# A merge gate whose last four weight tiles go bank by bank, with the merged tile's transposes among them and inside the second output projection

## The chip, the core and the metric

The kernel runs on one core of a Trainium2 chip. Its engines work side by side and meet only at semaphores: TensorE (PE) multiplies and accumulates into PSUM banks, ScalarE (ACT) applies activations and copies, VectorE (DVE) does elementwise work, GpSimd (POOL) as well, and SyncE (SP) issues the transfers. The metric is the device time of one execution in microseconds, lower is better; a kernel is given by the median of its runs.

## The reference

Two transformer blocks stand one after the other on 256 tokens of width 1024. The change lies in the second block, where two branches are gated and added, and the sum goes through an output projection:

```python
merged = jax.nn.sigmoid(g_a) * o_gla + jax.nn.sigmoid(g_b) * o_sgu
y = jnp.einsum('bte,ed->btd', merged, w_out[l])
x = x + gate1[:, None, :] * y
h2 = modulate(rms_norm_2(x, norm2_w[l]), shift2, scale2)
y2 = peer(h2, peer_w_q[l], peer_keys1[l], peer_keys2[l], peer_down[l], peer_up[l])
```

`g_a` and `g_b` are slices of one input projection `h @ w_in`; `o_gla` is the output of the gated linear attention, `o_sgu` that of the spatial gating unit. `peer` retrieves experts with a query projection `w_q`.

## The kernel before

All products are computed in float32 quality from two rounded parts. Each weight tile of 128 x 1024 goes through three engines: SP loads it into `raw` (`tile`, L326), ACT copies it rounded into `whi` (`hi`, L493), POOL subtracts to get the remainder `wlo` (`lo`, L431), and PE multiplies with both. There are four slots for each of the three (R = 4), and tile n uses slot n % 4. So the `hi` of tile n waits until PE has finished with tile n - 4 (`tile_used`) and the transfer of tile n has landed (`raw_full`); the `lo` waits for the `hi`; PE waits for the `lo`; and the transfer of tile n + 4 waits for the `lo` of tile n. ACT and POOL take the tiles strictly in order, with other work written between them by hand.

The second block's projections run as groups of eight tiles (k = 0 to 7), one for each 128 of the 1024 inputs. `m_tile` (L855) multiplies one tile into the four banks 0 to 3: bank b holds tokens 128 * (b // 2) onward and half b % 2 of the 1024 outputs, so a tile takes three matmuls for each bank (L867, L868, L869), twelve in all. The group `m_gb` computes `g_b` from the tiles called k0 to k7 below. `m_group_by_halves` runs the first six of them over all banks, then k6 and k7 over banks 0 and 1, then k6 and k7 over banks 2 and 3. As each bank is complete, ACT takes the sigmoid in place (L763), DVE multiplies by `msu` (L1767) and adds into `go` (L1768), the merged tile: two halves of 128 tokens, each of 1024 columns.

`go` must be transposed before the next product. PE transposes 128 x 128 blocks (`transposes`, L923), sixteen in all, into banks 4 to 7; the eight of the first 128 tokens stand ahead of the last tile of `m_gb` on banks 2 and 3, the eight of the other tokens after the group. Bank 4 + b then holds the inputs for tiles 2b and 2b + 1 of the next group: ACT copies it rounded into `xh` (`upper`, L523) and DVE subtracts to get `xl` (`turned`, L1309).

The group `wout2` is the output projection, from the tiles called w0 to w7 below (`m_group_by_halves` with the last three by halves: w0 to w4 over all banks, then w5 to w7 over banks 0 and 1, then over banks 2 and 3). DVE multiplies each finished bank by `gate1` (L1780) and adds into `xres` (L1783), between them it works on the conditioning tiles (`ada_tile`, L1344 and L1346), ACT and POOL make the norm, DVE scales (L1785), and PE transposes again (L923) and goes on to the query projection (`f_tile`, L849 to L851).

The order in which each engine meets its work is written out by hand. On ACT, around the change:

```python
his(T_IN2_M + 40 + 3, T_WOUT2 + 2)
...
    if b == 1:
        upper_of(T_WOUT2 + 2, T_WOUT2 + R - 1)
upper_of(T_WOUT2 + R - 1, T_WOUT2 + R)
upper("merged_T", first=4)
his(T_WOUT2 + R, T_WQ)
```

So ACT rounds w0 and w1 ahead of the first sigmoid, w2 after the second, w3 after the fourth, and only then the transposed banks. POOL's order is plain: `root` of the attention's norm (L450, L452) stands between k2 and k3, and from there on k3 to k7 and w0 to w7 follow each other.

Of the kernel before, what the change touches and what calls it, by code (L numbers as in the profile page):

```python
# [14 lines left out]
P = 128  # L15
# [38 lines left out]
def acc_freed(group, bank):  # L54

    before = GROUPS[:GROUPS.index(group)]
    if not before or group == "peer":
        return None
    if group == "in_M":
        return (("turned_lo", turn("mix", 4, 1)), ("gy_done", 1), ("ri_done", 1), ("ld_done", 1))[bank]  # L60
    if group == "wout":
        return (("turned_lo", turn("y", 4, 1)), ("turned_lo", turn("y", 4, 2)), ("a_raw", 6), ("a_pT", 6))[bank]
    last = before[-1]
    if last == "in2_T":
        return "xg_out", bank + 1
    if group == "merged_T":
        return "go_done", 1
    if group == "in2_T":
        return "unturned", scaled_at("in2", bank // 2 + 1)
    if last == "merged_T":  # L70
        return "unturned", scaled_at("merged", bank // 2 + 1)
    return ("turned_lo", turn(last[:-2], 4, bank + 1)) if last in TRANSPOSES else (READ_OUT[last], bank + 1)
# [22 lines left out]
Y_BANKS = [0, 1, 4, 5]  # L95

PAIRS = [(a, b) for a in range(16) for b in range(16) if (a + 1) * (b + 1) <= 16]
NPAIR = len(PAIRS)

TURNS = ["mix", "y", "mlp", "in2", "merged", "wq"]
SCALED = ["mix", "in2", "merged", "wq"]

# [11 lines left out]
def scaled_at(name, n):  # L116
    return 2 * SCALED.index(name) + n

# [24 lines left out]
def build(nc, x, stream, ada, cols, rows, lru_w, hgmask, causal, alibi, iota, walr, wup, sguw, keys, out):  # L143
    ctx = ExitStack()
    with ctx:
# [342 lines left out]
        def _(act):  # L488
# [28 lines left out]

            def upper(group, gains=None, first=0):

                for b in range(4):  # L520
                    act.wait_ge(acc_ready, acc_filled(group, b))
# [230 lines left out]
            for tt in range(TT):  # L752
                for h in range(4):
                    nc.scalar.activation(xn[:, tt, h * T:(h + 1) * T],
                                         bank[4 + 2 * tt + h // 2][:, (h % 2) * T:(h % 2 + 1) * T], ACT.Square,
                                         accum_out=gss[:, 4 * tt + h:4 * tt + h + 1]).then_inc(S("gla_ss"), 1)
            his(T_IN2_M + 40 + 3, T_WOUT2 + 2)
            for b in range(4):
                if b < 3:
                    act.wait_ge(acc_ready, acc_filled("m_gb", b))  # L760
                else:
                    act.wait_ge(tile_used, T_IN2_M + 48)
                nc.scalar.activation(bank[b][:, :], bank[b][:, :], ACT.Sigmoid).then_inc(S("gb_out"), 1)  # L763
                if b == 1:
                    upper_of(T_WOUT2 + 2, T_WOUT2 + R - 1)
            upper_of(T_WOUT2 + R - 1, T_WOUT2 + R)
            upper("merged_T", first=4)
            his(T_WOUT2 + R, T_WQ)
            upper_of(T_WQ, T_WQ + 1)
# [70 lines left out]
        def _(pe):  # L840
# [51 lines left out]

            def m_group_by_halves(a, group, twice, turned=None, before_last=lambda: None):
# [4 lines left out]
                for k in range(KC):  # L898
                    if turned and k % 2 == 0:
                        pe.wait_ge(S("turned_lo"), turn(turned, 4, k // 2 + 1))  # L900
                    if k < KC - twice:
                        tile(k, group=group if k == 0 else None)
                    else:
                        tile(k, banks=(0, 1), used=False)
                for k in range(KC - twice, KC):
                    if k == KC - 1:
                        before_last()
                    tile(k, banks=(2, 3))
# [280 lines left out]
            for tt in range(TT):  # L1189
                for h in range(4):  # L1190
# [98 lines left out]
        def _(v):  # L1289
# [13 lines left out]

            def turned(name, gains, first=0):

                for b in range(4):
                    v.wait_ge(S("turned_hi"), turn(name, 4, b + 1))
# [10 lines left out]
            def turned_shifted(group, name, gains, shifts):  # L1318

                for b in (0, 2):  # L1320
# [5 lines left out]
                    last.then_inc(S("affine"), 1)  # L1326
                turned(name, None)

            def ada_tile(n):
# [714 lines left out]
```

## Time and profile before

| | us |
|---|---|
| median of 3 runs | 1416.97 (1416.82 to 1417.31) |
| the profiled execution | 1417.1 |
| its span, first to last instruction | 1415.3 |
| outside the span | 1.8 |
| PE busy | 1369.9 (97%) |
| POOL busy | 1056.2 (75%) |
| DVE busy | 755.6 (53%) |
| ACT busy | 710.1 (50%) |
| mean granted TensorE clock | 0.987 of full speed |

A row of a timeline gives the start in microseconds from the span's start, the busy time, the engine, the line, the operation with its output and inputs, and how many instructions it merges; in brackets the idle time of the engine ahead of it and what ended that. The instructions of PE overlap, so the distance between two starts tells its pace, not the duration. A row of the stretch view gives for each engine the busy time and the number of instructions, then the granted clock as a share of full speed (1.00 is 2.4 GHz, 0.50 is 1.2 GHz), and the DMA engines' share and rate.

### The profile page before, as it was taken

What the parts mean: (1) busy time and instruction counts of PE and PEld (TensorE: products, weight loads), DVE (VectorE), ACT (ScalarE), POOL (GpSimd) and SP (SyncE); (2) the same over time, 40 slices, a digit from 0 to 9 for tenths busy, and PEclk for the clock granted to TensorE, in tenths of its full rate; (3) what the DMA queues carried; (4) which work ended last, traced back from release to release, by engine and by line L of the source; (5) the groups of instructions that cost most, each with busy time, mean ns of one, the idle gap of its engine ahead of it and who ended that gap; (6) DMA issues with size and microseconds to landing.
All of it is one profiled execution on the core that took longest, in us unless ns stands there. A gap on an engine that the chain in (4) does not pass through costs nothing.

```text
span 1415.3 us, 28941 instructions
## 1 busy us (share of the span) xinstructions
PE 1369.9 (97%) x9762; PEld 1219.6 (86%) x9762; DVE 755.6 (53%) x1616; ACT 710.1 (50%) x1129; POOL 1056.2 (75%) x469
## 2 busy tenths in 40 slices
PE   6998999999999998899999999999999999999997
PEld 6887899998877886899999999999977777788886
DVE  4655433334258526349991176666688888611113
ACT  6444555555345443435556543343355555556664
POOL 6554688886678885668888877777777777788885
PEclk9999999998999999999999999999999999999999
DMA  8443677774545456535555554444444445475552
GB/s 305 154 164 107 243 289 279 274 264 146 198 147 180 149 172 259 199 134 179 179 187 183 178 165 162 157 155 162 157 155 163 163 165 169 156 259 193 193 191 98
DMA packets 72651, 263.02 MB, mean 186 GB/s; under 512 B 8208, under 2 KB 9104, under 8 KB 72224
## 3 DMA queue, kind: packets, MB, share of 16 engines
q1 hardware_dynamic: 72608, 262.46, 53.6%
q8 instruction: 25, 0.41, 0.1%
q14 instruction: 18, 0.15, 0.0%
HBM read 259.81 MB, written 2.62 MB: 185 GB/s over the span
## 4 chain that ended last, share of the span: by engine, by line
PE 89%; DVE 5%; issue 2%; ACT 1%; POOL 1%; DMA 1%; SPq 0%; POOLq 0%; ACTq 0%; DVEq 0%
PE bank L849 14%; PE bank L867 14%; PE bank L850 14%; PE bank L851 14%; PE bank L868 13%; PE bank L869 13%; PE bank L1242 3%; DVE arena L1718 1%; DMA raw<-stream 1%; PE bank L965 1%; POOL wlo L431 1%; PE bank L1224 1%; PE bank L923 0%; DVE bank L1346 0%; PE bank L1154 0%
## 5 line engine op out<-in xcount | busy, mean ns | idle before, releaser
L431 POOL TENSOR_TENSOR wlo<-raw,whi 128x1024 fp32r<-128x1024 f32 x432 | 1041.8, 2423 | 315.5 <-ACT whi L493 312.4
L493 ACT ACTIVATE whi<-raw 128x1024 fp32r<-128x1024 f32 x432 | 455.7, 1057 | 350.9 <-PE bank L869 255.3
L849 PE MATMUL bank<-xh,whi 128*128 128x256 f32 x1600 | 462.2, 289 | 6.9 <-DVE xl L1314 4.5
L850 PE MATMUL bank<-xl,whi 128*128 128x256 f32 x1600 | 455.3, 285 | 0.0
L851 PE MATMUL bank<-xh,wlo 128*128 128x256 f32 x1600 | 455.0, 284 | 0.0
L867 PE MATMUL bank<-whi,xh 128*128 128x512 f32 x800 | 321.2, 402 | 9.7 <-DVE xl L1549 2.5
L849 PEld LDWEIGHTS bank<-xh,whi 128*128 128x128 f32 x1600 | 309.8, 194 | 12.0 <-POOL wlo L431 6.5
L868 PE MATMUL bank<-wlo,xh 128*128 128x512 f32 x800 | 313.2, 392 | 0.0
L869 PE MATMUL bank<-whi,xl 128*128 128x512 f32 x800 | 313.0, 391 | 0.0
L850 PEld LDWEIGHTS bank<-xl,whi 128*128 128x128 f32 x1600 | 310.0, 194 | 1.2
L851 PEld LDWEIGHTS bank<-xh,wlo 128*128 128x128 f32 x1600 | 309.5, 193 | 0.0
L867 PEld LDWEIGHTS bank<-whi,xh 128*128 128x128 f32 x800 | 151.1, 189 | 44.7 <-POOL wlo L431 4.9
L869 PEld LDWEIGHTS bank<-whi,xl 128*128 128x128 f32 x800 | 151.0, 189 | 32.0
L868 PEld LDWEIGHTS bank<-wlo,xh 128*128 128x128 f32 x800 | 151.2, 189 | 28.4
L789 ACT ACTIVATE arena<-bank 128x256 f32 x128 | 49.3, 385 | 180.9 <-PE bank L851 180.7
L1916 DVE TENSOR_TENSOR xl<-bank,xh 128x256 fp32r<-128x256 f32 x128 | 53.5, 418 | 143.5 <-ACT bank L816 143.5
L1901 DVE TENSOR_TENSOR xs<-bank,xs 128x768 bf16<-128x768 f32 x128 | 121.5, 949 | 0.0
L1909 DVE TENSOR_TENSOR arena<-arena,bank 128x256 f32 (+1 forms) x128 | 53.8, 421 | 102.1 <-PE bank L1242 101.9
L1899 DVE TENSOR_TENSOR ua<-xs,bank 128x512 bf16<-128x512 f32 (+1 forms) x128 | 87.0, 680 | 0.0
L1631 DVE TENSOR_TENSOR ul<-bank,uh 128x256 fp32r<-128x256 f32 x32 | 13.6, 425 | 120.2 <-ACT bank L676 120.2
L1242 PEld LDWEIGHTS bank<-xs,ua 128*128 128x128 bf16 x1536 | 51.9, 98 | 19.3 <-DVE xs L1901 15.7
L1242 PE MATMUL bank<-xs,ua 128*128 128x64 bf16 x1536 | 67.0, 194 | 0.0
(279 smaller groups left out, 1155.5 us busy)
## 6 DMA issues: line engine op xcount, KB each, us to landing
raw<-stream SPq DMA_DIRECT2D x432, 512.0 KB, 3.3
arena<-ada SPq DMA_DIRECT2D x48, 512.0 KB, 4.8
arena<-rows SPq DMA_DIRECT2D x5, 512.0 KB, 8.6
xs<-x SPq DMA_DIRECT2D x2, 512.0 KB, 4.6
arena<-rows SPq DMA_DIRECT2D x1, 1024.0 KB, 5.4
x_spill<-xs SPq DMA_DIRECT2D x1, 1024.0 KB, 6.2
xs<-x_spill SPq DMA_DIRECT2D x1, 1024.0 KB, 6.0
out<-arena SPq DMA_DIRECT2D x2, 512.0 KB, 2.6
```

The lines of the kernel that those rows point to most:

```text
L431: nc.gpsimd.tensor_tensor(wlo[:, slot, :], raw[:, slot, :], whi[:, slot, :].bitcast(F32), ALU.subtract).then_inc(lo_done, 1)
L493: nc.scalar.activation(whi[:, slot, :], raw[:, slot, :], ACT.Copy).then_inc(hi_done, 1)
L849: nc.tensor.matmul(dst, h_, xh[:, k, :], start=(k == 0), stop=False)
L850: nc.tensor.matmul(dst, h_, xl[:, k, :], start=False, stop=False)
L851: last = nc.tensor.matmul(dst, l_, xh[:, k, :], start=False, stop=(k == KC - 1))
L867: nc.tensor.matmul(bank[b][:, :], ah[:, ts], whi[:, slot, cs], start=start, stop=False)
L868: nc.tensor.matmul(bank[b][:, :], ah[:, ts], wlo[:, slot, cs], start=False, stop=False)
L869: last = nc.tensor.matmul(bank[b][:, :], al[:, ts], whi[:, slot, cs], start=False, stop=final)
L1242: last = nc.tensor.matmul(bank[6 + q % 2][:, t_ * HALF:(t_ + 1) * HALF], oneB[:, q % 2, t_, :], oneA[:, q % 2, part, t_, :], start=(part = ...
L1899: ttt(oneB[:, slot], bc(1, P), counts.to_broadcast([P, 4, P]), ALU.is_equal)
L1901: ttt(oneA[:, slot], same.unsqueeze(1).to_broadcast([P, 3, 4, HALF]), picks[:, 2:5, ts].unsqueeze(3).to_broadcast([P, 3, 4, HALF]), ALU.mu ...
L1909: ttt(dst, dst, bank[6 + q % 2][:, 0:4 * HALF].rearrange("p (t n) -> p n t", t=4), ALU.mult)\
```

## The change

PE now runs k0 to k3 over all banks, and then one bank after the other: bank 0 with k4 to k7, bank 1 with k4 to k7, bank 2, bank 3 (`m_group_by_banks`). Since a tile is given free with its last bank, k4 to k7 are given free only in bank 3. Transposes are issued in fours: tokens 0 to 127 for banks 4 and 5 ahead of bank 2, for banks 6 and 7 ahead of bank 3; tokens 128 to 255 for banks 4 and 5 ahead of the last tile in bank 3, for banks 6 and 7 between w0 and w1. `merged_out` counts the four finished pieces of `go` and takes the place of two steps of `unturned`; the banks 0 to 3 of `wout2` wait for it one by one. ACT and DVE follow: three sigmoids, w0, two transposed banks, the fourth sigmoid, w1, the other two transposed banks, w2 onward. DVE makes `xl` of the first two banks ahead of the fourth merge. Nothing is added or removed in arithmetic. The diff adds two functions that nothing calls (`upper_among`, `turned_among`); they are left out here, as are the renamings of `before_last`.

```diff
 def acc_freed(group, bank):
...
     if last == "merged_T":
-        return "unturned", scaled_at("merged", bank // 2 + 1)
+        return "merged_out", bank + 1
...
-SCALED = ["mix", "in2", "merged", "wq"]
+SCALED = ["mix", "in2", "wq"]
...
-            his(T_IN2_M + 40 + 3, T_WOUT2 + 2)
-            for b in range(4):
-                if b < 3:
-                    act.wait_ge(acc_ready, acc_filled("m_gb", b))
-                else:
-                    act.wait_ge(tile_used, T_IN2_M + 48)
+            his(T_IN2_M + 40 + 3, T_WOUT2)
+            for b in range(3):
+                act.wait_ge(acc_ready, acc_filled("m_gb", b))
                 nc.scalar.activation(bank[b][:, :], bank[b][:, :], ACT.Sigmoid).then_inc(S("gb_out"), 1)
-                if b == 1:
-                    upper_of(T_WOUT2 + 2, T_WOUT2 + R - 1)
-            upper_of(T_WOUT2 + R - 1, T_WOUT2 + R)
-            upper("merged_T", first=4)
-            his(T_WOUT2 + R, T_WQ)
+            upper_of(T_WOUT2, T_WOUT2 + 1)
+            upper("merged_T", first=4, banks=(0, 1))
+            act.wait_ge(tile_used, T_IN2_M + 48)
+            nc.scalar.activation(bank[3][:, :], bank[3][:, :], ACT.Sigmoid).then_inc(S("gb_out"), 1)
+            upper_of(T_WOUT2 + 1, T_WOUT2 + 2)
+            upper("merged_T", first=4, banks=(2, 3))
+            his(T_WOUT2 + 2, T_WQ)
...
+            def m_group_by_banks(a, group, late, turned=None, before=lambda k: None, within={}, ahead=lambda b, k: None):
...
+                for k in range(KC - late):
...
+                        tile(k, **kw)
+                for b in range(4):
+                    for k in range(KC - late, KC):
...
+                        ahead(b, k)
+                        tile(k, banks=(b,), used=b == 3)
+
+            def turn_of(group, src, ready, tt, bs):
+
+                for b in bs:
+                    pe.wait_ge(S(ready), 2 * tt + b // 2 + 1)
+                    if tt == 0:
+                        name, n = acc_freed(group, b)
+                        pe.wait_ge(S(name), n)
+                    for j in range(2):
+                        k = 2 * b + j
+                        last = nc.tensor.transpose(bank[turn_bank(group, b)][:, j * T + tt * P:j * T + (tt + 1) * P],
+                                                   src[:, tt, k * P:(k + 1) * P], ident[:, :])
+                    if tt:
+                        last.then_inc(acc_ready, 1)
...
-            m_group_by_halves(T_IN2_M + 40, "m_gb", 2,
-                              before_last=lambda: transposes("merged_T", "merged", go, first=4, tts=(0,)))
-            transposes("merged_T", "merged", go, first=4, tts=(1,))
-            m_group_by_halves(T_WOUT2, "wout2", 3, "merged")
+            def go_turn(b, k):
+                at = (b, k - KC)
+                if at in ((2, -4), (3, -4)):
+                    turn_of("merged_T", go, "merged_out", 0, (0, 1) if b == 2 else (2, 3))
+                if at == (3, -1):
+                    turn_of("merged_T", go, "merged_out", 1, (0, 1))
+
+            m_group_by_banks(T_IN2_M + 40, "m_gb", 4, ahead=go_turn)
+
+            def go_turn_rest(k):
+                if k == 1:
+                    turn_of("merged_T", go, "merged_out", 1, (2, 3))
+
+            m_group_by_halves(T_WOUT2, "wout2", 3, "merged", before=go_turn_rest)
...
-                last = ttt(go[:, tt, cs], go[:, tt, cs], bank[b][:, :], ALU.add)
-                last.then_inc(S("unturned"), 1) if b % 2 else own(last)
-            turned("merged", None, first=4)
+                ttt(go[:, tt, cs], go[:, tt, cs], bank[b][:, :], ALU.add).then_inc(S("merged_out"), 1)
+                if b == 2:
+                    turned("merged", None, first=4, banks=(0, 1))
+            turned("merged", None, first=4, banks=(2, 3))
```

The order of instructions on ACT, at the merge (`whi<-raw` is the `hi` of a tile, `bank<-bank` a sigmoid, `xh<-bank` a transposed bank). Before, where the rows `whi<-raw` from the top are k3 to k7, then w0 and w1:

```order
L493 ACTIVATE whi<-raw 128x1024 [waits tile_used,raw_full3]
L493 ACTIVATE whi<-raw 128x1024 [waits tile_used,raw_full0]
L493 ACTIVATE whi<-raw 128x1024 [waits tile_used,raw_full1]
L763 ACTIVATE bank<-bank 128x512 [waits acc_ready] x2
L493 ACTIVATE whi<-raw 128x1024 [waits tile_used,raw_full2]
L763 ACTIVATE bank<-bank 128x512 [waits acc_ready]
L763 ACTIVATE bank<-bank 128x512 [waits tile_used]
L493 ACTIVATE whi<-raw 128x1024 [waits tile_used,raw_full3]
L523 ACTIVATE xh<-bank 128x512 [waits acc_ready] x4
```

(The first row is k7.) In the changed kernel, from k7 on as well:

```order
L500 ACTIVATE whi<-raw 128x1024 [waits tile_used,raw_full3]
L777 ACTIVATE bank<-bank 128x512 [waits acc_ready] x3
L500 ACTIVATE whi<-raw 128x1024 [waits tile_used,raw_full0]
L540 ACTIVATE xh<-bank 128x512 [waits acc_ready] x2
L781 ACTIVATE bank<-bank 128x512 [waits tile_used]
L500 ACTIVATE whi<-raw 128x1024 [waits tile_used,raw_full1]
L540 ACTIVATE xh<-bank 128x512 [waits acc_ready] x2
```

The roundings of w0, w1 and w2, which stood ahead of the first or third sigmoid, now stand behind the third sigmoid, the fourth sigmoid and the last transposed bank.

PE at the end of `m_gb`, before: from k6 on bank 3 over the first run of transposes (`bank<-ident,arena` is a pair of them) to k7 on bank 2.

```order
L869 MATMUL bank3<-whi,xl 128x512
L923 MATMUL bank4<-ident,arena 128x128 x2
L923 MATMUL bank5<-ident,arena 128x128 x2
L923 MATMUL bank6<-ident,arena 128x128 x2
L923 MATMUL bank7<-ident,arena 128x128 x2
L867 MATMUL bank2<-whi,xh 128x512
L868 MATMUL bank2<-wlo,xh 128x512
```

In the changed kernel: from k6 on bank 3 over the third of the four runs to k7 on bank 3 and the first matmul of w0.

```order
L885 MATMUL bank3<-whi,xl 128x512
L941 MATMUL bank4<-ident,arena 128x128 x2
L941 MATMUL bank5<-ident,arena 128x128 x2
L883 MATMUL bank3<-whi,xh 128x512
L884 MATMUL bank3<-wlo,xh 128x512
L885 MATMUL bank3<-whi,xl 128x512
L883 MATMUL bank0<-whi,xh 128x512
```

What stood in two runs of eight transposes, the second of them between the last matmul of `m_gb` and the first of w0, is now in four runs of four, with matmuls on either side of each; no transpose stands directly ahead of w0.

## Rows read from the trace of the kernel before

**Rows 1.** The page: busy time of the engines.

```profile
PE 1369.9 (97%) x9762; PEld 1219.6 (86%) x9762; DVE 755.6 (53%) x1616; ACT 710.1 (50%) x1129; POOL 1056.2 (75%) x469
```

**Rows 2.** Timeline of PE, 509 to 545 us.

```profile
509.67 0.58 PE L867 MATMUL bank<-whi,xh 128*128 128x512 f32 x1
510.09 0.39 PE L868 MATMUL bank<-wlo,xh 128*128 128x512 f32 x1
...
530.06 0.39 PE L869 MATMUL bank<-whi,xl 128*128 128x512 f32 x1
531.97 1.10 PE L923 MATMUL bank<-ident,arena 128*128 128x128 f32 x8 [1.52 <-DVE arena L1768]
532.82 0.47 PE L867 MATMUL bank<-whi,xh 128*128 128x512 f32 x1
...
534.06 0.40 PE L869 MATMUL bank<-whi,xl 128*128 128x512 f32 x1
537.22 1.09 PE L923 MATMUL bank<-ident,arena 128*128 128x128 f32 x8 [2.77 <-DVE arena L1768]
539.07 0.50 PE L867 MATMUL bank<-whi,xh 128*128 128x512 f32 x1 [0.76 <-DVE xl L1309]
...
543.52 0.39 PE L867 MATMUL bank<-whi,xh 128*128 128x512 f32 x1
```

**Rows 3.** Timeline of POOL, 513 to 556 us.

```profile
513.23 0.20 POOL L450 TENSOR_SCALAR arena<-arena 128x8 f32<-128x8 f32 x1 [6.50 <-ACT arena L754]
...
515.13 18.93 POOL L431 TENSOR_TENSOR wlo<-raw,whi 128x1024 fp32r<-128x1024 f32 x8
...
544.92 2.42 POOL L431 TENSOR_TENSOR wlo<-raw,whi 128x1024 fp32r<-128x1024 f32 x1 [6.45 <-ACT whi L493]
...
555.82 2.40 POOL L431 TENSOR_TENSOR wlo<-raw,whi 128x1024 fp32r<-128x1024 f32 x1 [0.32 <-ACT whi L493]
```

**Rows 4.** Timeline of ACT, 522 to 544 us.

```profile
522.60 1.06 ACT L493 ACTIVATE whi<-raw 128x1024 fp32r<-128x1024 f32 x1 [3.23 <-DMA raw<-stream]
...
528.45 1.26 ACT L763 ACTIVATE bank<-bank 128x512 f32<-128x512 f32 x2 [0.53 <-PE bank L869]
...
533.80 1.28 ACT L763 ACTIVATE bank<-bank 128x512 f32<-128x512 f32 x2 [2.19 <-PE bank L869]
...
537.69 2.07 ACT L523 ACTIVATE xh<-bank 128x512 fp32r<-128x512 f32 x4 [1.66 <-PE bank L923]
543.78 1.06 ACT L493 ACTIVATE whi<-raw 128x1024 fp32r<-128x1024 f32 x1 [4.02 <-PE bank L869]
```

**Rows 5.** Timeline of DVE, 529 to 561 us.

```profile
529.16 0.70 DVE L1767 TENSOR_TENSOR bank<-bank,arena 128x512 f32<-128x512 f32 x1 [10.67 <-ACT bank L763]
529.90 0.69 DVE L1768 TENSOR_TENSOR arena<-arena,bank 128x512 f32<-128x512 f32 x1
...
538.32 2.48 DVE L1309 TENSOR_TENSOR xl<-bank,xh 128x512 fp32r<-128x512 f32 x4 [1.16 <-ACT xh L523]
...
558.02 0.70 DVE L1780 TENSOR_TENSOR bank<-bank,arena 128x512 f32<-128x512 f32 x1 [7.39 <-PE bank L869]
...
560.69 2.40 DVE L1346 SCALAR_TENSOR_TENSOR bank<-arena,st,bank 128x512 f32<-128x512 f32 x3
```

**Rows 6.** Stretches at the lower clock (start:end, then each engine).

```profile
457.60:460.80 3.20, 3.20 (x9) 2.47 (x8) 3.20 (x5) 2.22 (x4) 0.00 (x0) 0.50 0.00 0
539.50:542.80 3.30, 3.30 (x10) 2.52 (x9) 3.12 (x6) 0.26 (x1) 0.00 (x0) 0.50 0.57 209
...
572.80:577.00 4.20, 4.20 (x20) 4.20 (x21) 2.93 (x5) 1.58 (x4) 1.54 (x1) 0.50 0.71 208
```

**Rows 7.** Timeline of PE ahead of the first of these stretches.

```profile
456.71 0.47 PE L867 MATMUL bank<-whi,xh 128*128 128x512 f32 x1 [2.04 <-DVE arena L1690]
```

**Rows 8.** Transfers issued from 527 to 560 us: count, size, median us to landing.

```profile
raw<-stream SPq DMA_DIRECT2D x10, 512.0 KB, 4.6
arena<-ada SPq DMA_DIRECT2D x8, 512.0 KB, 6.0
```

More of the change, by code:

```diff
@@ L95, with turn_bank @@
 Y_BANKS = [0, 1, 4, 5]
+T_BANKS = [4, 5, 0, 1]
+def turn_bank(group, b):
+    return 4 + b if group == "merged_T" else T_BANKS[b]
 PAIRS = [(a, b) for a in range(16) for b in range(16) if (a + 1) * (b + 1) <= 16]
@@ L516, in halves, with upper_among, upper @@
                 return [(2 * b + j, bank[b][:, j * T:(j + 1) * T]) for j in range(2)]
-            def upper(group, gains=None, first=0):
+            def upper_among(group, gains):
                 for b in range(4):
+                    act.wait_ge(acc_ready, acc_filled(group, b))
+                    for j in range(2):
+                        k = 2 * b + j
+                        last = nc.scalar.activation(xh[:, k, :], bank[T_BANKS[b]][:, j * T:(j + 1) * T], ACT.Copy,
+                                                    scale=gains[:, k:k + 1])
+                    last.then_inc(S("turned_hi"), 1)
+            def upper(group, gains=None, first=0, banks=range(4)):
+                for b in banks:
                     act.wait_ge(acc_ready, acc_filled(group, b))
@@ L891, in m_group, with tile, m_group_by_halves @@
                         part()
-            def m_group_by_halves(a, group, twice, turned=None, before_last=lambda: None):
+            def m_group_by_banks(a, group, late, turned=None, before=lambda k: None, within={}, ahead=lambda b, k: None):
+                def tile(k, **kw):
+                    m_tile((a + k) % R, a + k + 1, xh[:, k, :], xl[:, k, :], final=(k == KC - 1), **kw)
+                for k in range(KC - late):
+                    before(k)
+                    if turned and k % 2 == 0:
+                        pe.wait_ge(S("turned_lo"), turn(turned, 4, k // 2 + 1))
+                    kw = dict(group=group if k == 0 else None)
+                    if k in within:
+                        tile(k, banks=(0, 1), used=False, **kw)
+                        within[k]()
+                        tile(k, banks=(2, 3), **kw)
+                    else:
+                        tile(k, **kw)
+                for b in range(4):
+                    for k in range(KC - late, KC):
+                        if turned and b == 0 and k % 2 == 0:
+                            pe.wait_ge(S("turned_lo"), turn(turned, 4, k // 2 + 1))
+                        ahead(b, k)
[6 more added lines that the diff above has]
+                        pe.wait_ge(S(name), n)
+                    for j in range(2):
+                        k = 2 * b + j
+                        last = nc.tensor.transpose(bank[turn_bank(group, b)][:, j * T + tt * P:j * T + (tt + 1) * P],
+                                                   src[:, tt, k * P:(k + 1) * P], ident[:, :])
+                    if tt:
+                        last.then_inc(acc_ready, 1)
+            def m_group_by_halves(a, group, twice, turned=None, before=lambda k: None):
                 def tile(k, **kw):
@@ L898, in m_group_by_halves @@
                 for k in range(KC):
+                    before(k)
                     if turned and k % 2 == 0:
@@ L905, in m_group_by_halves @@
                 for k in range(KC - twice, KC):
-                    if k == KC - 1:
-                        before_last()
                     tile(k, banks=(2, 3))
@@ L1302, in scaled, with turned @@
                     tsc(xn[:, tt, :], xres[:, tt, :], rs(key, tt), None, ALU.mult).then_inc(S("unturned"), 1)
-            def turned(name, gains, first=0):
-                for b in range(4):
+            def turned(name, gains, first=0, banks=range(4)):
+                for b in banks:
                     v.wait_ge(S("turned_hi"), turn(name, 4, b + 1))
@@ L1327, in turned_shifted, with turned_among @@
                 turned(name, None)
+            def turned_among(name, gains):
+                for b in range(4):
+                    v.wait_ge(S("turned_hi"), turn(name, 4, b + 1))
+                    for j in range(2):
+                        k = 2 * b + j
+                        last = stt(xl[:, k, :], bank[T_BANKS[b]][:, j * T:(j + 1) * T], gains[:, k:k + 1],
+                                   xh[:, k, :].bitcast(F32), ALU.mult, ALU.subtract)
+                    last.then_inc(S("turned_lo"), 1)
             def ada_tile(n):
```

## Prediction

> **What bounds the kernel now.** I read the page first: PE is busy for 1369.9 of the span's 1415.3 us [rows 1], so the only thing to be won or lost here is time in which PE waits or runs at its lower clock. Then I read PE's own timeline over the merge, and after it the timelines of ACT, POOL and DVE over the same stretch, to see who ends each wait.
>
> PE's timeline [rows 2] shows 88 steps from 510.09 to 530.06, so one matmul takes 0.227 us; a tile on one bank (three matmuls) takes 0.68, a whole tile (or four tiles on one bank) 2.72. Then PE waits 1.52 us before the first eight transposes and 2.77 before the second eight, both ended by DVE's last merge (L1768), and 0.76 before w0, ended by DVE's `xl`. w0 starts at 539.07 and its twelve matmuls last until 543.52, 4.45 instead of 2.72 us, because from 539.5 to 542.8 the granted clock is 0.50, the level of 1.2 GHz [rows 6]. Waits and slow clock together come to 6.8 us. From 543.52 PE goes on without a gap: bank 0 of `wout2` would be complete 63 steps later, at 557.8, and DVE starts on it at 558.02 [rows 5]. That moment is what I compare, since from there DVE carries the chain (the two products, then the last conditioning tiles, at 560.69) into the norm and the next projection.
>
> The other engines show how tiles are supplied. POOL leaves the norm at 515.13 and then makes eight `lo` back to back in 18.93 us, 2.37 each [rows 3]: k3 to k7 and w0, w1, w2. POOL is behind there, not waiting. **So before the change w0, w1 and w2 are ready by 534.1, five microseconds before PE wants w0.**
>
> **What the change removes.** The three waits (5.05 us) and the slow start of w0 (1.73 us) have no cause left in their old form: the fourth merge is only wanted by w0's bank 3, and the merges of banks 0, 1 and 2 have matmuls of the following bank over them. The cover holds: a bank's last matmul ends 0.2 us before its sigmoid, DVE's product starts 0.71 after that (528.45 to 529.16), its sum at 529.90 takes 0.69 [rows 4, 5], so a piece of `go` is ready 2.3 us after its bank. Bank 3's k4 to k6 plus four transposes take 2.04 + 0.42 = 2.46 (eight transposes take 531.97 to 532.82, 0.85). That is enough by a tenth.
>
> **What it adds, first: four tiles are wanted in the time of one.** k0 to k3 end at 510.09 + 47 x 0.227 = 520.76. Bank 0 then wants k4, k5, k6, k7 at 0.68 us apart, but POOL delivers k4 at 519.86, k5 at 522.23, k6 at 524.59, k7 at 526.96 (515.13 plus two to five times 2.37). POOL is saturated, so nothing brings them earlier. PE waits 0.8 + 1.7 + 1.7 = 4.2 us and ends bank 0 at 527.7. Then bank 1 to 530.4, transposes and bank 2 to 533.55, transposes to 533.97, k4 to k6 on bank 3 to 536.0, transposes to 536.4, k7 to 537.1. Before, `m_gb` ended at 534.06 + 0.23 = 534.3.
>
> **Second: the next tiles are supplied late.** k4 to k7 are given free only in bank 3, k4 at 534.65. From a freed slot to the finished `lo` I take what w4 shows: w0 ends at 543.52, `hi` starts at 543.78, `lo` at 544.92 and takes 2.42 [rows 2, 3, 4], 3.82 us in all. So w0 is ready at 538.5, and PE waits 1.4 us for it. POOL, saturated before, now stands idle from 526.96 to 536.0. The `xl` that w0 needs is out by 537.9 (ACT takes two banks in 1.04, DVE 0.62 a bank [rows 4, 5]) and is covered. w0 runs to 541.2 and its bank 3 wants the fourth merge at 540.5; ACT starts that sigmoid at 537.5 behind two copies, DVE is done by 539.8: covered. Four transposes end at 541.65. On ACT the `hi` of w1 stands behind the fourth sigmoid (538.2 to 539.2), so its `lo` ends at 541.7: no wait worth naming. **The `hi` of w2 stands behind the copies of the last two transposed banks**, which start at 541.7: `hi` 542.75 to 543.8, `lo` to 546.3, while w1 ends at 544.5. PE waits 1.85. w2 starts at 546.3.
>
> **Third: POOL then has no lead left.** From 543.9 it makes w2 to w7 in a row, 2.37 to 2.40 each: w7 is ready at 558.1 to 558.3. PE does w2, w3, w4 (8.16), then w5, w6 on two banks (2.72) and wants w7 at 557.2: a wait of 1.0. Bank 0 is complete at 558.9, against 557.8. The transfers don't decide: each of w4 to w7 is issued when the `lo` four tiles earlier ends (w4 at 538.5, the earliest w7 at 548.7) and lands 4.6 us later [rows 8], ahead of its `hi`. The conditioning tiles issued behind w7's transfer land at about 555 by the 6.0 of [rows 8], and DVE's 3.2 us on them end at 558, one microsecond ahead of bank 0; a later landing would cost what it exceeds that by, 0 to 1.
>
> **The sum without the clock.** Gone: 5.05 us of waits in brackets and 1.73 of slow clock. A wait in brackets begins where the last matmul's record ends, 0.39 us after its start, though the next could have started after 0.227; so three waits cost 3 x 0.16 = 0.5 more, 7.3 in all. New, counted from pace to pace: 4.2 + 1.4 + 0.1 + 1.85 + 1.0 = 8.55. The transposes cost the same 1.7. 8.55 - 7.3 is 1.25, and the walk gives 558.9 - 557.8 = 1.1; I take **+1.1**.
>
> **The clock.** Whether it falls is open from both sides. It fell to 0.50 after PE had waited 2.04 us once [rows 6, 7], and at 539.5 only after waits of 1.52, 2.77 and 0.76 in 9 us. The new waits in bank 0 are 1.7 and 1.7 with 0.68 us of matmuls between, near both. A stretch of 3.4 us at the lower clock costs at most half of it, 1.7, and nothing while PE waits; with k7's matmuls and bank 1 in it I take 1.0 and a little over one in two that it comes. The other way: at the query projection PE restarts at 0.50 until 577.0 [rows 6]. If that stretch ends at the same instant, whatever delay reaches the restart is halved; if it moves along, nothing comes back. So 0 to half of the delay is returned; I take a quarter to a third. 1.1 + 0.6 - 0.4 = **+1.3 us**.
>
> The profiled execution took 1417.1, 0.1 above the median of 1416.97; the sum is a difference within it, and I put it on the median: **1418.3**. A measurement of this kernel can tell about 0.2%, 2.8 us, from no change, so I call the forecast no change.
>
> **Rivals.** Slower: the lower clock comes more than once. Place: the waits in bank 0 and those before w0 and w2. For it speaks that both known falls followed waits of this size [rows 2, 6, 7]; against it that between 530 and 539 only one came of three. Price: two stretches in full, 3.4, and nothing returned: 1.1 + 3.4 = +4.5, 1421.5. It decides from 1.7 us of slow clock upward (1.1 + 1.7 = 2.8). The Trainium skill ("TensorE: Matmul & The Clock Gate", the section "A second HAM failure mode: psum-queue depth-cycling") says that matmul groups that cycle through PSUM banks with frequent small pauses make the clock go up and down, and that this is paid between the bursts. By that rule the time would be this rival's, 1421.5, and by [rows 2, 6] alone the forecast's: the trace agrees only in part.
>
> Faster: PE finds k5 to k7 ready after all, because POOL has a lead that I don't see or takes less than 2.37 for each. Then the 4.2 us go: 1.1 - 4.2 = -3.1, 1413.9. [Rows 3] speaks against it: eight in a row with no gap. It would take a POOL that had begun at least 3 us earlier.
>
> Nothing for nothing: w7's wait isn't there, the clock doesn't fall, and the walk ends at +0.1, 1417.1. This is the lower part of the forecast, and within no change, as is the case that the transposes are simply off the path.
>
> **How the numbers follow.** Forecast with its lower part, +0.1 to +2.8: 0.68. Slower rival: 0.21. Faster rival: 0.11, more than [rows 3] gives it, since a walk of so many steps may miss one. Of the faster rival a part stays within 0.2%, of the slower one too, and I leave these against each other. Range: from 1415.2, which cuts off most of the faster rival, to 1421.0, which takes in +1.1 with a stretch and a half of slow clock (2.6) and 0.3 for a late transfer. Chances: faster by over 0.2% 0.11, within 0.68, slower 0.21.
>
> **What would show it.** In the changed profile: three waits of PE on POOL's `lo` (L438) between 521 and 527 of 0.8, 1.7 and 1.7; POOL idle for about 9 us from 527, ended by ACT; w0's first matmul at 538.5, w2's at 546.3 after 1.8 of wait on POOL; a wait of about 1 before w7; DVE on bank 0 of `wout2` at about 559; the granted clock at 0.50 somewhere in 524 to 531 or not. It is wrong if PE's waits in bank 0 sum to under 2 us, if any wait is ended by DVE's merge with over half a microsecond, or if the clock is low for over 7 us between 520 and 550.

## The result, and the profile after

| kernel | median us | lowest to highest | runs |
|---|---|---|---|
| before | 1416.81 | 1416.18 to 1417.31 | 8 |
| with the change | 1421.31 | 1418.27 to 1422.23 | 8 |

The ratio is 1.003, with a 95% interval of 1.0021 to 1.0038: the change makes the kernel slower by 0.3%, 4.5 us in the medians. The forecast was 1418.3, no change, with a range up to 1421.0. The profiled execution took 1421.53 us, its span is 1419.7, and its mean granted clock 0.984. The page of the changed kernel, for [rows 1]:

```profile
span 1419.7 us, 28944 instructions
PE 1372.9 (97%) x9762; PEld 1220.7 (86%) x9762; DVE 756.0 (53%) x1616; ACT 709.6 (50%) x1129; POOL 1055.5 (74%) x469
PE 39%; POOL 31%; issue 22%; DVE 5%; DMA 1%; ACT 1%; POOLq 1%; SPq 0%; ACTq 0%; DVEq 0%
```

PE is busy for 3.0 us more with the same number of matmuls, so part of the loss is not waiting but slower matmuls. The third line is the split of the chain that ended last: POOL has 31% of it, where before it had 1% (and PE 89%). Nearly all of that lies behind 560 us, where the distance between the two kernels does not grow for hundreds of microseconds (below), so it is no measure of the loss at the merge.

PE's timeline over the merge, for [rows 2] (start us, us, engine, line, operation, then in brackets the idle time before it and what ended it):

```profile
520.93 0.50 PE L883 MATMUL bank<-whi,xh 128*128 128x512 f32 x1 [0.67 <-POOL wlo L438]
521.27 0.39 PE L884 MATMUL bank<-wlo,xh 128*128 128x512 f32 x1
...
523.25 0.50 PE L883 MATMUL bank<-whi,xh 128*128 128x512 f32 x1 [1.36 <-POOL wlo L438]
...
525.57 0.79 PE L883 MATMUL bank<-whi,xh 128*128 128x512 f32 x1 [1.33 <-POOL wlo L438]
526.16 0.63 PE L884 MATMUL bank<-wlo,xh 128*128 128x512 f32 x1
526.59 0.63 PE L885 MATMUL bank<-whi,xl 128*128 128x512 f32 x1
...
531.34 0.39 PE L885 MATMUL bank<-whi,xl 128*128 128x512 f32 x1
531.57 0.60 PE L941 MATMUL bank<-ident,arena 128*128 128x128 f32 x4
531.92 0.48 PE L883 MATMUL bank<-whi,xh 128*128 128x512 f32 x1
532.24 0.40 PE L884 MATMUL bank<-wlo,xh 128*128 128x512 f32 x1
...
539.78 0.47 PE L883 MATMUL bank<-whi,xh 128*128 128x512 f32 x1 [1.17 <-DVE xl L1371]
...
547.64 0.47 PE L883 MATMUL bank<-whi,xh 128*128 128x512 f32 x1 [1.71 <-POOL wlo L438]
```

The three waits of bank 0 are there, for k5, k6 and k7; no transpose waits. The rows from 525.57 are what the forecast had too small: matmuls 0.43 us apart instead of 0.227. The same stretch by windows (length, then busy time of PE, PEld, DVE, ACT and POOL, the granted clock, the transfers' share and GB/s), for [rows 6]:

```profile
517.00:524.00 7.00, 4.97 (x21) 3.34 (x19) 0.13 (x1) 2.08 (x2) 7.00 (x4) 1.00 0.67 223
524.06:530.89 6.83, 5.50 (x14) 4.16 (x14) 1.39 (x2) 0.58 (x1) 1.45 (x1) 0.50 0.78 257
530.89:545.00 14.11, 12.94 (x65) 10.43 (x64) 6.68 (x11) 6.76 (x11) 4.75 (x2) 1.00 0.46 165
1032.65:1036.06 3.41, 3.41 (x15) 2.37 (x14) 3.29 (x7) 0.77 (x3) 0.05 (x1) 0.50 0.46 154
```

The clock is at 0.50, the level of 1.2 GHz, for 6.83 us, twice the 3.4 of [rows 6]. It falls at 524.06, between the second and the third wait, so only the waits of 0.67 and 1.36 us stand ahead of the fall. The last row is a second stretch, 500 us later, that the trace of before does not have.

POOL's timeline over the merge, for [rows 3]:

```profile
511.87 0.20 POOL L457 TENSOR_SCALAR arena<-arena 128x8 f32<-128x8 f32 x1 [6.50 <-ACT arena L771]
...
513.76 11.75 POOL L438 TENSOR_TENSOR wlo<-raw,whi 128x1024 fp32r<-128x1024 f32 x5
537.32 2.36 POOL L438 TENSOR_TENSOR wlo<-raw,whi 128x1024 fp32r<-128x1024 f32 x1 [11.80 <-ACT whi L500]
540.34 2.39 POOL L438 TENSOR_TENSOR wlo<-raw,whi 128x1024 fp32r<-128x1024 f32 x1 [0.66 <-ACT whi L500]
545.12 16.52 POOL L438 TENSOR_TENSOR wlo<-raw,whi 128x1024 fp32r<-128x1024 f32 x7 [2.39 <-ACT whi L500]
```

ACT's, for [rows 4]:

```profile
543.00 1.08 ACT L540 ACTIVATE xh<-bank 128x512 fp32r<-128x512 f32 x2 [2.74 <-PE bank L941]
543.97 3.90 ACT L500 ACTIVATE whi<-raw 128x1024 fp32r<-128x1024 f32 x4
```

And DVE's, for [rows 5]:

```profile
527.97 0.70 DVE L1839 TENSOR_TENSOR bank<-bank,arena 128x512 f32<-128x512 f32 x1 [10.84 <-ACT bank L777]
...
538.35 1.29 DVE L1371 TENSOR_TENSOR xl<-bank,xh 128x512 fp32r<-128x512 f32 x2 [1.34 <-ACT xh L540]
...
554.86 0.75 DVE L1416 TENSOR_SCALAR bank<-arena,st 128x512 f32<-128x512 f32 x1 [3.42 <-DMA arena<-ada]
...
560.33 0.70 DVE L1853 TENSOR_TENSOR bank<-bank,arena 128x512 f32<-128x512 f32 x1 [2.27 <-PE bank L885]
```

POOL makes five `lo` in a row, stands idle for 11.80 us and then has seven in a row with no lead. On ACT the `hi` of w2, the first of the four at 543.97, stands behind the two copies at 543.00, which wait for PE's last transposes; that is where w2's wait comes from. The wait before w0 is put down to DVE's `xl`, but DVE's first bank of it was out by 539.0 and POOL's `lo` of w0 only at 537.32 + 2.36 = 539.68, a tenth of a microsecond before the matmul, so POOL's end is the later one.

**Where the time went.** This execution is ahead of the one of before by 1.3 us already ahead of the merge (POOL's root at 511.87 against 513.23 [rows 3]), which has nothing to do with the change. So I measure from a mark ahead of it: from ACT's first square of the attention norm, at 510.11 before and 508.76 after, to DVE's first product on bank 0 of `wout2`. That is 47.91 us before and 51.57 after: **+3.66 us at the merge**. The mark before and after:

```profile
510.11 0.39 ACT L754 ACTIVATE arena<-bank 128x256 f32<-128x256 f32 x1 [4.64 <-PE bank L1195]
508.76 0.38 ACT L771 ACTIVATE arena<-bank 128x256 f32<-128x256 f32 x1 [4.64 <-PE bank L1247]
```

Four hundred us further on, at the DVE instruction that stands 1200 from the end, the distances are 440.44 and 444.08, +3.64: all of it is passed on. The span's difference is 4.4: -1.3 from the start, +3.6, +1.6 over the stretch at 1032 (the difference of the distances is 3.64 ahead of it and 5.24 at the DVE instruction 800 from the end), and 0.5 behind that.

### The profile page after: what moved, and what is told of

Same layout as the page of the kernel before. It is cut to its first block, busy times and chain, and to the rows that moved or that the text cites. A ratio compares the mean times of both kernels' runs of the same rounds, so it can differ in the third digit from the quotient of the medians.

```text
span 1419.7 us, 28944 instructions
## 1 busy us (share of the span) xinstructions
PE 1372.9 (97%) x9762; PEld 1220.7 (86%) x9762; DVE 756.0 (53%) x1616; ACT 709.6 (50%) x1129; POOL 1055.5 (74%) x469
## 4 chain that ended last, share of the span: by engine, by line
PE 39%; POOL 31%; issue 22%; DVE 5%; DMA 1%; ACT 1%; POOLq 1%; SPq 0%; ACTq 0%; DVEq 0%
POOL wlo L438 30%; PE bank L883 8%; PE bank L884 8%; PE bank L885 8%; PE bank L865 4%; PE bank L867 4%; PE bank L866 4%; DMA raw<-stream 1%; DVE arena L1790 1%; PE bank L1017 1%; DVE bank L1418 0%; POOLq L437 0%; POOLq L442 0%; PE bank L975 0%; PE bank L1206 0%
```

## Experiments

The clock theory: the three short waits of bank 0 bring the clock down, and this is the loss beyond the walk of the prediction. Its rivals: the tiles come later than I walked (the walk), or the waits before w0, w2 and w7 carry the loss (the supply after the merge). Distances are from the first square to DVE's first product, "late" is the distance to the later DVE instruction, both against before (47.91 and 440.44). The median of before was 1416.81 beside the change, 1417.12 beside fill_waits, w2_early, root_later and late_two, and 1417.02 beside the other four. The last column is the mean over all runs of a kernel of the granted clock that each run shows; for before it is 0.9871 over 64 runs.

| kernel | median us | ratio to before, 95% interval | merge | late | clock at 0.50 near the merge | mean clock, all runs |
|---|---|---|---|---|---|---|
| the change | 1421.31 | 1.003 (1.0021 to 1.0038) | +3.66 | +3.64 | 6.83 us | 0.9853 |
| fill_waits | 1418.56 | 1.0016 (1.0007 to 1.0025) | +1.31 | +2.11 | none | 0.9884 |
| w2_early | 1420.05 | 1.0015 (1.0005 to 1.0025) | +1.69 | +1.10 | 6.83 us | 0.9854 |
| root_later | 1419.58 | 1.0015 (1.0006 to 1.0024) | +1.48 | +2.23 | 3.41 us | 0.9865 |
| late_two | 1412.47 | 0.9969 (0.996 to 0.9978) | -5.45 | -4.78 | none | 0.9879 |
| both | 1415.93 | 0.9992 (0.9983 to 1.0) | -1.03 | -0.94 | none | 0.9888 |
| late_three | 1415.07 | 0.9981 (0.9973 to 0.999) | -3.12 | -3.18 | none | 0.9875 |
| before_busy | 1415.59 | 0.9988 (0.9979 to 0.9996) | -1.62 | -0.80 | none | 0.9884 |
| two_busy | 1411.34 | 0.9957 (0.9945 to 0.9969) | -5.51 | -6.80 | none | 0.9907 |

Where "late" differs from "merge", the difference arises at one place, the restart of PE at the query projection, between 562 and 580 us. The clock is at 0.50 there for 6.83 us in eight of the ten traces, but the stretch begins sooner or later against the matmuls: in the change it covers 16 matmuls of the projection, in before 21, in fill_waits, root_later, late_two and before_busy 28 or 29, which lose 0.7 to 0.8 us there against before. In w2_early it lasts 3.41 us, which gives 0.6 back:

```profile
574.06:577.47 3.41, 2.82 (x13) 2.85 (x14) 2.63 (x5) 2.18 (x5) 2.14 (x1) 0.50 0.58 169
```

So the merge column is the one that shows an experiment's effect, but for two_busy, whose edit stands at the restart; the late column and the medians have this scatter on top.

**The waits filled with matmuls that nobody reads.** Same order of tiles and same waits for POOL; PE works in them.

```
+            def filler(slot, n):
+                pe.wait_ge(S("go_done"), 1)
+                for _i in range(n):
+                    nc.tensor.matmul(bank[7][:, :], xh[:, 0, 0:P], whi[:, slot, 0:512], start=True, stop=True)
...
                         ahead(b, k)
+                        if b == 0 and k > KC - late:
+                            filler((a + k - 1) % R, n=3 if k == KC - late + 1 else 6)
```

> The change, with 3, 6 and 6 matmuls into bank 7, whose result nobody reads, ahead of k5, k6 and k7 in bank 0 of m_gb, which is shorter than the waits there. Clock theory: the granted clock stays at 1.00 from 520 to 535 though PE still gets k5 to k7 no earlier; the 2.7 us that 5.3 us at half the clock cost go: 1418.6. Supply theory alone (the clock is nothing): the same 1421.3, as the tiles come no sooner.

Its PE timeline and windows over the merge:

```profile
518.96 0.84 PE L913 MATMUL bank<-whi,xh 128*128 128x512 f32 x3
...
520.61 1.55 PE L913 MATMUL bank<-whi,xh 128*128 128x512 f32 x6
...
522.97 1.53 PE L913 MATMUL bank<-whi,xh 128*128 128x512 f32 x6
524.52 0.50 PE L883 MATMUL bank<-whi,xh 128*128 128x512 f32 x1
...
536.26 0.47 PE L883 MATMUL bank<-whi,xh 128*128 128x512 f32 x1 [1.18 <-DVE xl L1379]
```

```profile
517.00:524.00 7.00, 6.98 (x30) 5.13 (x29) 0.00 (x0) 1.06 (x1) 7.00 (x4) 1.00 0.65 218
524.00:531.00 7.00, 6.98 (x33) 5.47 (x32) 2.77 (x4) 1.16 (x2) 0.47 (x1) 1.00 0.83 310
```

The clock stays at 1.00 and the distance falls by 2.35 us, 51.57 to 49.22, though k5, k6 and k7 start 2.36 us apart (519.81, 522.17, 524.52), no closer than in the change (2.32). The median falls by 2.75. What is left is +1.31, beside the walk's +1.1. So the clock theory holds, and the tiles came as walked. The traces are one execution each, but the runs agree: the mean clock is 0.9884 over the eleven runs here and 0.9853 over the eight of the change, which is about 9 us less at 0.50 (twice the difference, times 1418 us). POOL's idle time is also 9.32 us here, the "about 9" of the prediction.

**The `hi` of w2 ahead of the copies of the last two transposed banks.**

```
-            upper_of(T_WOUT2 + 1, T_WOUT2 + 2)
+            upper_of(T_WOUT2 + 1, T_WOUT2 + 3)
             upper("merged_T", first=4, banks=(2, 3))
-            his(T_WOUT2 + 2, T_WQ)
+            his(T_WOUT2 + 3, T_WQ)
```

> The change, with the rounding of w2 on ACT moved ahead of the last two transposed banks. Supply theory: the wait before w2 (1.71 us in the changed kernel's trace, with 0.16 of overlap) shrinks to a few tenths, and w7's (0.55) goes with it, since POOL keeps its lead; 2.4 us less than the change, 1418.9. Rival, only the lower clock costs anything: the waits are slack and the time stays at 1421.3. Rival, the time outside the merge decides (the stretch at 1032 us): no difference either.

The wait before w2 is gone, the waits of bank 0 are 0.69, 1.35 and 1.35 as in the change, and the clock falls for 6.83 us all the same. The distance falls by 1.97 us. The wait lies on the path, and that queue on ACT costs what the supply theory says; but it leaves the clock as it was, so it is not what brought it down. In the runs the gain over the change is 1.3 us in the medians (2.4 were expected), with single runs from 1415.3 to 1421.1; the two fastest show a clock of 0.989, the eight above 1419 one of 0.982 to 0.986.

**One wait of bank 0 fewer.** k3's `hi` goes ahead of the squares on ACT, and two more `lo` ahead of the root on POOL.

```
-            los(T_IN2_M + 8 + R - 1, T_IN2_M + 40 + R - 1)
+            los(T_IN2_M + 8 + R - 1, T_IN2_M + 40 + R + 1)
             root(S("gla_ss"), 8, gss, grs, 1.0 / 256)
-            los(T_IN2_M + 40 + R - 1, T_WQ + 1)
+            los(T_IN2_M + 40 + R + 1, T_WQ + 1)
...
+            upper_of(T_IN2_M + 40 + 3, T_IN2_M + 40 + 4)
...
-            his(T_IN2_M + 40 + 3, T_WOUT2)
+            his(T_IN2_M + 40 + 4, T_WOUT2)
```

> The change, with k3 and k4 rounded and made on ACT and POOL ahead of the attention's norm instead of behind it, so that POOL works in the 6.5 us in which it waited for that norm's sums. Supply theory: k5, k6, k7 come about 2 us earlier, the waits in bank 0 fall from 4.0 to about 2 us, and the clock may then stay up: 1417.0 to 1419.3. Rival, the supply is set by transfers (ACT's round of k7 waited 3.57 us for one): nothing changes at k7, 1421.3.

```profile
522.67 0.50 PE L884 MATMUL bank<-whi,xh 128*128 128x512 f32 x1 [1.05 <-POOL wlo L438]
...
524.98 0.79 PE L884 MATMUL bank<-whi,xh 128*128 128x512 f32 x1 [1.35 <-POOL wlo L438]
```

Two waits are left, 2.4 us instead of 3.4. The clock still falls, from 524.89, but for 3.41 us instead of 6.83, and the distance is 2.18 us shorter than the change's. k7 comes 1.3 us earlier from the mark (15.54 against 16.81), not the 2 expected, because POOL still waits 3.04 us for the `hi` of k4, which ACT makes behind the squares; that it comes earlier at all speaks against the transfers as what sets the supply. The lead is worth the wait it removes (about 1.1) and half of the slow stretch (about 1.1). A lead of 1.3 us, half a tile, was not enough to keep the clock, and the median of 1419.58 lies just above the 1417.0 to 1419.3 expected.

**Two tiles by banks instead of four.** The middle way between the two kernels: only k6 and k7 go bank by bank, so w0 and w1 are supplied early again.

```
-                if at in ((2, -4), (3, -4)):
-                    turn_of("merged_T", go, "merged_out", 0, (0, 1) if b == 2 else (2, 3))
-                if at == (3, -1):
-                    turn_of("merged_T", go, "merged_out", 1, (0, 1))
+                if at in ((3, -2), (3, -1)):
+                    turn_of("merged_T", go, "merged_out", 0, (0, 1) if k == KC - 2 else (2, 3))
 
-            m_group_by_banks(T_IN2_M + 40, "m_gb", 4, ahead=go_turn)
+            m_group_by_banks(T_IN2_M + 40, "m_gb", 2, ahead=go_turn)
+            turn_of("merged_T", go, "merged_out", 1, (0, 1))
```

On ACT the `hi` of w0 and w1 go ahead of the first sigmoid, w2's behind the third, w3's behind the fourth.

> Only k6 and k7 bank by bank, k0 to k5 over all banks; the first transposes ahead of k6 and of k7 on bank 3, the third four right behind the group; ACT rounds w0 and w1 ahead of the first sigmoid as before the change, w2 and w3 around the fourth. Supply theory: no wait on POOL in bank 0 or at w0, one wait of about 1.7 for DVE's xl before w0, no lower clock in m_gb: bank 0 of wout2 about 5.7 us earlier than before the change, 1411.1. Rival, the merge chain is what costs and bank by bank is no gain: between before and the change, 1417 to 1421.

```profile
530.79 0.66 PE L941 MATMUL bank<-ident,arena 128*128 128x128 f32 x4
532.64 0.50 PE L883 MATMUL bank<-whi,xh 128*128 128x512 f32 x1 [1.19 <-DVE xl L1370]
```

```profile
513.03 16.57 POOL L438 TENSOR_TENSOR wlo<-raw,whi 128x1024 fp32r<-128x1024 f32 x7
531.01 2.37 POOL L438 TENSOR_TENSOR wlo<-raw,whi 128x1024 fp32r<-128x1024 f32 x1 [1.41 <-ACT whi L500]
```

POOL makes seven `lo` in a row instead of five and then idles for 1.41 us instead of 11.80. Over the merge PE waits once, 1.19, and the clock stays at 1.00. 5.45 us are gained on before and 9.11 on the change; the median is 1412.47, faster than before by 0.31%. The idea of the change is good, its depth was not: the loss lay in taking four tiles for it. The depth and ACT's order change together here: with four late tiles k4's slot is free only in bank 3, so w0 can't be rounded ahead of the sigmoids.

**The two mends at once, with four tiles kept** (the fillers and w2's early `hi`):

> The change with both edits: fillers in bank 0's waits and w2 rounded ahead of the last copies. Theory (slow clock 2.4 and w2's wait 2.0 are separate terms of the 3.7 us that the merge lost): from the first square on ACT to DVE's first product of wout2 47.2 to 47.5 us, 0.4 to 0.7 less than before the change (47.91); time 1416.5. Rival, one lives off the other (with the fillers the wait before w2 is covered anyway): as with the fillers alone, 49.2 and 1418.6.

The distance is 46.88, 1.03 less than before, and the runs are at 0.9992 (0.9983 to 1.0). The mends add up: 51.57 - 2.35 - 1.97 = 47.25, and the trace is 0.37 better still; w7's wait is 0.21 here, 0.54 with the fillers alone. Without slow clock and without w2's wait, four tiles are no worse than before, and no better that can be measured. Late_two's 42.46 is 4.4 us less, about the 3.8 of bank 0's waits, which the fillers hide from the clock but don't remove, and the 0.4 of w7's.

**Three tiles by banks.** The first transposes stand ahead of k5 and k6 on bank 3, the third four behind the group; ACT rounds w0 ahead of the first sigmoid, w1 behind the third and w2 behind the fourth.

> As late_two, but k5, k6 and k7 bank by bank, and w1 rounded behind bank 3's k5. Supply theory, by POOL's pace of 2.37 us a tile: waits of 0.4 and 1.7 us in bank 0, w0 about 2 us later than in late_two, so 44.4 to 45 us from the first square to DVE's first product (late_two 42.46) and 1414.5, more if the clock falls. Rival, the bank order itself costs nothing and only four tiles overrun the ring: as late_two, 1412.5.

```profile
524.16 0.50 PE L883 MATMUL bank<-whi,xh 128*128 128x512 f32 x1 [0.32 <-POOL wlo L438]
...
526.48 0.50 PE L883 MATMUL bank<-whi,xh 128*128 128x512 f32 x1 [1.36 <-POOL wlo L438]
```

-3.12 at the merge, between two tiles (-5.45) and four. Here one wait of 1.36 with one of 0.32 ahead of it left the clock at 1.00, where root_later's 1.05 and 1.35 did not: one profiled execution each, so this is where it turned here and not a rule. How little one execution says shows at the 2.04 us wait of [rows 7]: it stands in `both` as well, at 454.48, and there the clock stays at 1.00, where in the other nine traces it falls for 3.41 us.

**The kernel before with its waits filled.** Six matmuls of 512 columns ahead of the first eight transposes and 24 of 128 columns ahead of the second eight; nothing of the change in it.

```
-            m_group_by_halves(T_IN2_M + 40, "m_gb", 2,
-                              before_last=lambda: transposes("merged_T", "merged", go, first=4, tts=(0,)))
+            def busy(dst, cols, slot, n):
...
+            def first_turn():
+                busy(bank[7][:, :], 512, (T_IN2_M + 47) % R, 6)
+                transposes("merged_T", "merged", go, first=4, tts=(0,))
+            m_group_by_halves(T_IN2_M + 40, "m_gb", 2, before_last=first_turn)
+            pe.wait_ge(lo_done, T_WOUT2 + 3)
+            busy(bank[7][:, 128:256], 128, (T_WOUT2 + 2) % R, 24)
             transposes("merged_T", "merged", go, first=4, tts=(1,))
```

> The kernel before the change, with matmuls whose results nobody reads in its waits ahead of the two runs of transposes (6 of 512 columns, 24 of 128). Clock theory: the waits stay, the stretch at 0.50 from 539.4 to 542.8 goes, w0 takes 2.7 instead of 4.45 us: 46.2 us from the first square to DVE's first product instead of 47.91, and 1415.4. Rival, the clock fell for another reason than the idle time: no change, 1417.1.

```profile
532.30 1.10 PE L923 MATMUL bank<-ident,arena 128*128 128x128 f32 x8 [0.16 <-DVE arena L1779]
...
534.62 2.79 PE L1202 MATMUL bank<-whi,xh 128*128 128x128 f32 x24
...
539.40 0.51 PE L867 MATMUL bank<-whi,xh 128*128 128x512 f32 x1 [0.76 <-DVE xl L1320]
```

No slow stretch, w0 to w1 at full pace, and 1.62 us less, the 1.73 that the prediction read as w0's slow start. In the median 1.4 us and in the late distance 0.80: about the size, close to what the runs can tell. The clock's price is shown in both kernels. It also splits late_two's gain of 5.45: 1.6 are before's slow stretch, which late_two doesn't have, and 3.8 (46.29 less 42.46) are the order itself; and the four tiles of `both`, at 46.88, are 0.6 behind this kernel.

**Two tiles by banks, and PE kept busy at the query projection.** Ten and eight matmuls into bank 4 around the transposes of `wq`, against late_two:

```
-            transposes("wq_T", "wq", xn)
+            def busy(count, slot, n):
+                pe.wait_ge(lo_done, count)
+                for _i in range(n):
+                    nc.tensor.matmul(bank[4][:, :], whi[:, slot, 0:P], whi[:, slot, 0:512], start=True, stop=True)
+            transposes("wq_T", "wq", xn, tts=(0,))
+            busy(T_WQ + 1, T_WQ % R, 10)
+            transposes("wq_T", "wq", xn, tts=(1,))
+            busy(T_WQ + 1, T_WQ % R, 8)
```

> late_two, with 10 and 8 matmuls whose results nobody reads in the two waits of the transposes and of the first tile ahead of the query projection (2.45 and 2.21 us in late_two's trace), at a place that the change doesn't touch. Clock theory: the stretch at 0.50 of 6.8 us there goes, of which about 5.7 lie in matmuls: 2.8 us less than late_two, 1409.7. Rival, waits of that size keep the clock low whatever stands in them, or the fillers run over and delay the first tile: 1412.5 or more.

Late_two's two waits and its stretch at 0.50:

```profile
561.94 1.09 PE L975 MATMUL bank<-ident,arena 128*128 128x128 f32 x8 [2.45 <-DVE arena L1857]
565.25 0.55 PE L865 MATMUL bank<-xh,whi 128*128 128x256 f32 x1 [2.21 <-DVE xl L1370]
564.18:571.00 6.82, 5.75 (x27) 5.79 (x28) 4.12 (x8) 2.91 (x7) 2.61 (x2) 0.50 0.72 219
```

The same place in two_busy:

```profile
561.20 2.54 PE L1270 MATMUL bank<-whi 128*128 128x512 f32 x10
563.90 1.09 PE L975 MATMUL bank<-ident,arena 128*128 128x128 f32 x8 [0.15 <-DVE arena L1866]
564.75 2.09 PE L1270 MATMUL bank<-whi 128*128 128x512 f32 x8
567.21 0.35 PE L865 MATMUL bank<-xh,whi 128*128 128x256 f32 x1 [0.37 <-DVE xl L1379]
...
569.18 0.39 PE L865 MATMUL bank<-xh,whi 128*128 128x256 f32 x1 [0.30 <-DVE xl L1379]
```

The restart is at full clock, and 2.0 us of the 2.8 expected come: from the first square to ACT's table load in the query projection 115.16 us against 117.17. The rest is a new wait: at full pace PE runs into DVE's `xl` (0.37 and 0.30). It is the fastest kernel here, 1411.34, which is 0.43% below before, and its interval of 0.9945 to 0.9969 excludes before and the change; that it beats late_two is shown at this place only (the medians are 1.1 apart, on different chips).

## Why the prediction was wrong

- **What goes** (5.05 of waits, 1.73 of slow start): right. No transpose waits after the change, and w0 runs at full pace.
- **First, bank 0's supply** (0.8 + 1.7 + 1.7 = 4.2): right in place and releaser. Measured are 0.67, 1.36 and 1.33, and each is 0.16 more from pace to pace: 3.8.
- **Second and third, the later supply**: right, with POOL's idle time one of the signs (9.32 without the slow clock; 11.80 with it). w0 1.17 + 0.16 for 1.4, w2 1.71 + 0.16 for 1.85, w7 0.55 + 0.16 for 1.0. The wait that the prediction gave w1 (0.1) isn't there. The conditioning tiles were late by 3.42 on DVE and were still done 2.27 ahead of bank 0, as walked, and the merges stayed covered.
- **The sum without the clock** (+1.1): right. 3.66 less the 2.5 of slow clock (below) is 1.2, and fill_waits shows 1.31. By the terms the waits came to 0.8 less than the 8.55 taken, so the right sum is in part two misses that cancel. What I had left out makes up for it: after a wait or a turn the first two matmuls start 0.34 or 0.31 apart, not 0.227 (520.93 to 521.27, 531.92 to 532.24), some 0.1 us a place. The change has ten such places up to w7 on bank 0, before has two, w0 and the first run of transposes: about 0.8 us more.
- **The clock: the step that failed.** The term for the lower clock was sized at +0.6 us: one stretch of 3.4 us at a cost of 1.0, "a little over one in two that it comes". It came, 6.83 us long, and nearly all its time lay in matmuls: from 525.57 to 531.34 fourteen paces take 5.77 us, where 0.34 + 13 x 0.227 = 3.29 are usual, so 2.5 us were lost where 0.6 stood in the sum. The length was the larger error: I had read the only stretch at the merge [rows 6] as the size of any, though the restart's was longer in the same rows. Nor is the length a property of the code: at about 153 us, far ahead of the change, the stretch is 6.83 us long in seven of the ten traces and 3.41 in fill_waits, late_two and `both`. With the same three waits it was 6.83 us twice, in the change and in w2_early. The prediction's own sign for this, a low clock for over 7 us between 520 and 550, was set too wide to catch it.
- **What is returned at the restart** (-0.4): nothing. The delay is +3.66 ahead of it and +3.64 far behind: the stretch of the restart moved along (570.16 to 576.99 before, 571.85 to 578.68 after, 6.83 us each). The other kernels show how much of that is chance: from the merge to behind the restart they go from 0.6 us returned (w2_early) to 0.8 us lost (fill_waits, before_busy).
- **The slower rival** (two stretches in full, nothing returned, +4.5) gave 1421.5, and 1421.31 was measured. It was right in mechanism and in the first of its two places, bank 0, as one stretch of double length; I gave it 0.21. That its time fits to 0.2 us is luck: it priced the clock at 3.4 us, of which the merge shows 2.5, and the rest comes from elsewhere (below). The rule that the prediction cites from the Trainium skill ("TensorE: Matmul & The Clock Gate", "A second HAM failure mode: psum-queue depth-cycling") spoke for it, and the trace agrees in that the clock fell among short pauses between groups of matmuls (0.67 and 1.36 us). It differs in that the groups stay on one bank and the pauses are waits for POOL.
- **The range** ended 0.3 below the result. Three runs of before spread over 0.5 us, and I read that as the scatter. Over 35 and 29 later runs before lay between 1414.1 and 1419.3, and the kernels here spread by 3 to 6 us. Whether a slow stretch comes, or comes twice, seems to be part of it: the profile of the change has the one at 1032 us, w2_early's has it too (1031.44 to 1034.86), and none of the others has one behind 600 us, apart from the one in which every trace ends. What brings it, 500 us behind the change in code that is the same, stays open. It may make up the 0.9 us between 3.6 at the merge and 4.5 in the medians, an estimate from the mean clocks: 0.98525 against 0.98713 is about 5.3 us more at 0.50, of which the merge explains 6.83 - 3.41 = 3.4; the other 1.9 would cost up to 1.0 us. No run shows it directly.

## What to carry to other kernels

Before work is cut into banks so that its consumers can start early, count how many weight tiles the first bank then wants in the time of one, against the pace and the lead of the engine that makes them: here two tiles gained 5.5 us at the merge (1.6 of it a slow stretch that went with the old order), three gained 3.1 and four lost 3.7, each with ACT's order fitted to it. When PE must wait several times in short order, price the lower clock over the matmuls behind the waits in full, not as an afterthought; and where waits can't be removed, matmuls with an unread result in a free bank kept the clock up at their place in all four kernels here that had them; they must end before what they cover does. Compare two profiles from a mark ahead of the change, not from the span's start.

## What the runs showed of the hardware

- The clock fell to 0.50 after waits of 0.67 and 1.36 us and ahead of a third of 1.33, with 1.0 us of matmuls between them, with no single idle time over 1.4, and for 6.83 us; with 1.05 and 1.35 it fell for 3.41, 0.1 us ahead of the end of the second, with 0.32 and 1.36 not at all, and with the same waits filled not at all (PE busy for 6.98 of 7.00 us).
- After one wait of 2.04 us [rows 7] it fell for 3.41 us in nine traces and stayed at 1.00 in the tenth (`both`).
- At 0.50 a matmul of 512 columns starts every 0.43 us instead of 0.227, one of 256 columns every 0.21 instead of 0.12.
- In late_two eight transposes stood between waits of 2.45 and 2.21 us, and the clock fell at 564.18, inside the second wait; the same transposes with matmuls around them, in two_busy, were followed by a clock of 1.00 throughout 555 to 580 us.
